# Attention blocks copied within SBUF by many small transfers of the load queue, and bias diagonals issued in other slots

## What is computed

```python
DIL_CONFIGS = ((128, 1), (512, 4), (2048, 16))   # window, dilation
HEADS_A, HEAD_DIM = 16, 64
qkv = (h @ w_qkv).reshape(B, T, N_GROUPS_A, 3, HEADS_A, HEAD_DIM)
for g, (window, dilation) in enumerate(DIL_CONFIGS):
    o, l = dilated_group_attention(qkv[:, :, g, 0], qkv[:, :, g, 1], qkv[:, :, g, 2],
                                   window, dilation, rel_table)
    ...
alpha = jax.nn.softmax(jnp.stack(lses, axis=0), axis=0)
o = jnp.sum(alpha[..., None] * jnp.stack(outs, axis=0), axis=0)
return o.reshape(B, T, D_MODEL) @ w_o
```

## Time and profile before

| | us |
|---|---|
| median of 3 runs | 1636.84 |
| the 3 runs | 1634.02 to 1636.91 |
| the profiled execution | 1637.76 |
| its span, first to last instruction | 1635.8 |
| mean granted TensorE clock | 0.986 |
| PE busy | 1590.2 (97%) |

### The profile page before, as it was taken

How to read it: one execution, slowest core, us unless ns; L and a number is a source line. 1 busy time by engine, 2 the same in 40 slices (tenths; PEclk the granted TensorE clock), 3 DMA queues, 4 the chain that set the end, 5 groups by cost and what they waited for, 6 DMA issues and landing times.

```text
span 1635.8 us, 21746 instructions
## 1 busy us (share of the span) xinstructions
PE 1590.2 (97%) x8034; PEld 1305.4 (80%) x8034; DVE 919.4 (56%) x1585; ACT 591.5 (36%) x1064; POOL 143.2 (9%) x208
## 2 busy tenths in 40 slices
PE   9999899899899999999999999999999999999998
PEld 7878678687688878888888887888878888888887
DVE  5456365464565774444545576776776353545565
ACT  5314233133133432222223345666653222222344
POOL 2020120211201110000000110000020000000111
PEclk9999899999999999999999999999999999999999
DMA  5574574755744333333333333233223333333332
GB/s 162 149 213 129 152 200 119 205 137 164 191 128 137 112 88 93 91 103 90 102 91 102 107 100 104 68 99 99 59 84 94 103 91 102 93 100 92 101 105 75
DMA packets 309980, 189.48 MB, mean 116 GB/s; under 512 B 33786, under 2 KB 297523, under 8 KB 309923
## 3 DMA queue, kind: packets, MB, share of 16 engines
q1 hardware_dynamic: 300112, 158.61, 33.9%
q0 software_dynamic: 9552, 30.08, 6.7%
q10 hardware_dynamic: 258, 0.04, 0.0%
HBM read 171.79 MB, written 25.28 MB: 120 GB/s over the span
## 4 chain that ended last, share of the span: by engine, by line
PE 87%; DMA 5%; SPq 2%; DVE 2%; POOL 1%; ACT 1%; issue 1%; ACTq 0%; POOLq 0%; DVEq 0%
PE unit_out L1704 24%; PE unit_out L1705 23%; PE unit_out L1706 23%; DMA w_raw<-in_a_w_qkv_dram 5%; SPq L747 2%; PE attn L1852 2%; POOL sumsq L912 1%; DVE w_lo L1238 1%; PE attn L2100 1%; PE turned L1780 1%; PE unit_out L1871 1%; PE unit_out L1872 1%; PE unit_out L1873 1%; PE logits L1704 1%; ACT w_hi L930 1%
## 5 line engine op out<-in xcount | busy, mean ns | idle before, releaser
L1704 PE MATMUL unit_out<-act_hi,w_hi 128*128 128x512 f32 x1849 | 732.1, 396 | 32.2 <-DVE w_lo L1238 30.7
L1706 PE MATMUL unit_out<-act_hi,w_lo 128*128 128x512 f32 x1849 | 723.4, 391 | 0.0
L1705 PE MATMUL unit_out<-act_lo,w_hi 128*128 128x512 f32 x1849 | 723.2, 391 | 0.0
L930 ACT ACTIVATE w_hi<-w_raw 128x1024 fp32r<-128x1024 f32 (+3 forms) x256 | 271.0, 1058 | 508.3 <-PE unit_out L1706 352.3
L1704 PEld LDWEIGHTS unit_out<-act_hi,w_hi 128*128 128x128 f32 x1849 | 350.6, 190 | 111.4 <-DVE w_lo L1238 36.8
L1706 PEld LDWEIGHTS unit_out<-act_hi,w_lo 128*128 128x128 f32 x1849 | 350.2, 189 | 73.8
L1705 PEld LDWEIGHTS unit_out<-act_lo,w_hi 128*128 128x128 f32 x1849 | 350.7, 190 | 70.4 <-issue 0.2
L1238 DVE TENSOR_TENSOR w_lo<-w_raw,w_hi 128x1024 fp32r<-128x1024 f32 (+3 forms) x256 | 319.7, 1249 | 146.2 <-ACT w_hi L930 145.9
L912 POOL TENSOR_TENSOR sumsq<-sumsq,square 128x512 f32<-128x512 f32 x41 | 57.8, 1411 | 1057.9 <-ACT square L958 1056.2
L1100 ACT ACTIVATE act_hi<-hidden 128x512 fp32r<-128x512 f32 x64 | 40.5, 633 | 243.4 <-DVE hidden L1502 243.4
L1499 DVE TENSOR_TENSOR scaled<-unit_out,rstd 128x512 f32<-128x512 f32 x62 | 42.8, 690 | 67.7 <-PE unit_out L1706 67.7
(11 more groups left out here) (297 smaller groups left out, 1388.5 us busy)
## 6 DMA issues: line engine op xcount, KB each, us to landing
w_raw<-in_w_ff_dram SPq DMA_DIRECT2D x128, 512.0 KB, 4.0
w_raw<-in_a_w_qkv_dram SPq DMA_DIRECT2D x56, 512.0 KB, 4.3
turned_blocks<-blocks POOLq DMA_DIRECT2D x28, 512.0 KB, 5.4
probs<-turned_blocks POOLq DMA_DIRECT2D x112, 128.0 KB, 4.1
w_raw<-in_b_w_qkv_dram SPq DMA_DIRECT2D x24, 512.0 KB, 4.9
w_raw<-in_a_w_qkv_dram SPq DMA_DIRECT2D x32, 256.0 KB, 3.9
w_raw<-in_w_ple_gate_dram SPq DMA_DIRECT2D x16, 512.0 KB, 3.9
bias_tiles_b<-bias_vectors SPq DMA_DIRECT2D x16, 256.0 KB, 5.1
```

What stands on the lines that cost most here:

```text
L930: sc.activation(weights_of(u)[0][:, 0:width, :], w_raw[par][:, 0:width, :], ACT.Copy).then_inc(hi_done, 1)
L1704: te.matmul(bank, w_k[0], hi, start=start, stop=False)
L1705: te.matmul(bank, w_k[0], lo, start=False, stop=False)
L1706: return te.matmul(bank, w_k[1], hi, start=False, stop=stop)
```

## The change

The tensor `turned_blocks` and POOL's loop go. In their place SP issues, for each phase, 16 transfers straight from `blocks` to `probs[ph]`, each of 32 rows x 256 floats (32 KB), with one wait for `blocks_ready` ahead of them (`spread_blocks`). They stand behind the loads of slots 6, 7, 8 and of slot 0 of the next step; the last of these in step 7 is behind the first load of `w_o`, which is therefore issued within the loop (`load_out_slab`). PE waits for 16 x 16 instead of 16 x 4 on `probs_landed`. The ten bias diagonals of `expand_a` are issued by head: five behind slot 4, five behind slot 5. `expand_b` stands in slots 2, 3 and 5.

```diff
+EXPAND_AT = {4: (0,), 5: (1,)}
+SPREAD_BEHIND = {6: 0, 7: 1, 8: 2, 0: 3}
-TILES_B_AT = [A_UNITS * step + slot for step in range(1, A_PAIRS) for slot in (0, 4, 8)][:HEADS]
+TILES_B_AT = [A_UNITS * step + slot for step in range(1, A_PAIRS) for slot in (2, 3, 5)][:HEADS]
...
-            def expand_a(pair):
+            def expand_a(pair, halves=(0, 1)):
...
-                for h in (2 * pair, 2 * pair + 1):
+                for h in [2 * pair + half for half in halves]:
...
-            for u in range(2, A_PAIRS * A_UNITS):
-                load_a(At(u // A_UNITS), At(u), u % A_UNITS)
+            def spread_blocks(step, n):
+
+                ph = A_TURN_ORDER[n]
+                sp.wait_ge(blocks_ready, A_ITEMS * (step - 1) + n + 1)
+                for i, j in itertools.product(range(NT), range(NT)):
+                    sp.dma_start(turned_order(probs[ph][j * SUB:(j + 1) * SUB, :])[:, i, :],
+                                 turned_order(blocks[i * SUB:(i + 1) * SUB, ph, :])[:, j, :]
+                                 ).then_inc(probs_landed[ph], 16)
+
+            for u in range(2, A_PAIRS * A_UNITS + 1):
+                if u < A_PAIRS * A_UNITS:
+                    load_a(At(u // A_UNITS), At(u), u % A_UNITS)
+                else:
+                    load_out_slab(U_AO, 0, a_w_o[0], u - U_AO)
+                slot = u % A_UNITS
+                step = u // A_UNITS - (slot == 0)
+                if slot in SPREAD_BEHIND and step > 0:
+                    spread_blocks(step, SPREAD_BEHIND[slot])
+                if u >= A_PAIRS * A_UNITS:
+                    continue
...
-                if u == 8 or u > A_UNITS and u % A_UNITS == 6 and u // A_UNITS < A_PAIRS - 1:
-                    expand_a(u // A_UNITS + 1)
+                if u == 8:
+                    expand_a(1)
+                if u > A_UNITS and u % A_UNITS in EXPAND_AT and u // A_UNITS < A_PAIRS - 1:
+                    expand_a(u // A_UNITS + 1, EXPAND_AT[u % A_UNITS])
...
-            for n in range(A_ITEMS * (A_PAIRS - 1)):
-                ph = A_TURN_ORDER[n % A_ITEMS]
-                pool.wait_ge(blocks_ready, n + 1)
-                pool.dma_start(blocks_d.ap()[ph], blocks[:, ph, :]).then_inc(blocks_stored, 16)
-                pool.wait_ge(blocks_stored, 16 * (n + 1))
-                for j in range(NT):
-                    pool.dma_start(turned_order(probs[ph][j * SUB:(j + 1) * SUB, :]),
-                                   blocks_d.ap()[ph].rearrange("(i k) (j c) -> k j i c", i=NT, j=NT)[:, j]
-                                   ).then_inc(probs_landed[ph], 16)
...
-                            wait(te, probs_landed[ph], s.times(16 * NT))
+                            wait(te, probs_landed[ph], s.times(16 * NT * NT))
```

More of the change, by code:

```diff
@@ L349, in build @@
         tiles_b = nc.dram_tensor("bias_tiles_b", (HEADS, P, T), F32, kind="Internal")
-        blocks_d = nc.dram_tensor("turned_blocks", (A_ITEMS, P, 2 * T), F32, kind="Internal")
         unit_out = [ps(f"unit_out{i}", [P, T]) for i in range(2)]
@@ L616, in build @@
         blocks_ready = sem("blocks_ready")
-        blocks_stored = sem("blocks_stored")
         probs_landed = [sem(f"probs_landed{i}") for i in range(A_ITEMS)]
@@ L776, in expand_b, with load_out_slab @@
                                      [[VEC, HEADS], [-1, P // HEADS], [1, T]])).then_inc(tiles_b_ready, 16)
-            for u in range(2, A_PAIRS * A_UNITS):
-                load_a(At(u // A_UNITS), At(u), u % A_UNITS)
+            def load_out_slab(first, layer, w_o, n):
+                load(At(first + n), w_o.rearrange("(k p) c -> p k c", p=P)[:, 0:KC - LATE[layer], n * P:(n + 1) * P])
+            def spread_blocks(step, n):
[16 more added lines that the diff above has]
+                    continue
                 if u == 3:
@@ L786, in _, with load_out @@
                     load_bias_a(u // A_UNITS)
-                if u == 8 or u > A_UNITS and u % A_UNITS == 6 and u // A_UNITS < A_PAIRS - 1:
-                    expand_a(u // A_UNITS + 1)
+                if u == 8:
+                    expand_a(1)
+                if u > A_UNITS and u % A_UNITS in EXPAND_AT and u // A_UNITS < A_PAIRS - 1:
+                    expand_a(u // A_UNITS + 1, EXPAND_AT[u % A_UNITS])
                 if u in TILES_B_AT:
                     expand_b(TILES_B_AT.index(u))
-            def load_out(first, layer, w_o):
+            def load_out(first, layer, w_o, done=0):
                 late = LATE[layer]
                 view = w_o.rearrange("(k p) c -> p k c", p=P)
-                for n in range(KC):
-                    load(At(first + n), view[:, 0:KC - late, n * P:(n + 1) * P])
+                for n in range(done, KC):
+                    load_out_slab(first, layer, w_o, n)
                 for i in range(late):
@@ L822, in load_gate @@
                                      ).then_inc(proj_raw_ready[par], 16)
-            load_out(U_AO, 0, a_w_o[0])
+            load_out(U_AO, 0, a_w_o[0], 1)
             sp.wait_ge(logits_done, ITEMS_A)
```

## The result

The changed kernel takes 1702.8 us (median of 4, 1701.45 to 1704.84) against 1635.9 of the kernel before (median of 4): a ratio of 1.0411, interval 1.0393 to 1.0429. The forecast was 1599 with a range of 1589 to 1638. The case that came true is rival C, SP as the bound, and it cost more than the 1671 given for it.

A forecast was written before the change was run, and what follows sets the result against it. PE was bound by six waits for weight loads issued late behind ten bias diagonals. 1637.8 - 45.4 (waits gone) + 7 (copies on SP) = 1599.4, with the median 0.9 lower: 1599 us, range 1589 to 1638.

The forecast's parts named there:

- rival C: SP becomes the bound; fourth phase's copies land 9.0 us late per step at pitch 0.60; 1671 us, chance 0.17.
- What bounds the kernel: PE, steps 1 to 6: six waits for late weight loads cost 45.4 us, 30.7 idle and 14.7 low clock.
- Diagonals split: Five diagonals behind slot 4, five behind slot 5: all six waits gone, -45.4 us; other bound about -13.
- Copies: Sixteen SP issues per phase at pitch 0.475 us; PE waits 1.0 us at the values product, seven times: +7 us.
- The upper bound of 0.60: Copy issue pitch on SP taken from the diagonals, instead of 0.475; would make PE wait 9.0 us a step.
- The working that went with it: SP falls behind 2.1 us per phase; step 7's last copies land at 516.0, wanted at 515.0; waiting begins at pitch 0.46.
- Low clock: Behind each PE wait the clock drops to 1.2 GHz, costing 2.4 us per wait beyond the idle time.
- The wait for `blocks_ready` on SP: Holds SP for nothing, since DVE transposes each phase just ahead of the `w_lo` that allows the preceding load.
- Up to 2 us of lag from the diagonals: If diagonals still hold SP when slot 6 is due, up to 2 us more per step, +12 us.
- The rules of the Trainium skill that speak against the change: Under 64 KB mostly overhead; more issuing engines save just issue time, which the change gives up, sized by the pitch.
- 33 us for sixteen copies: Time of a phase's copies run one after another by the skill page's fit; the prediction held that rows speak against it.

The follow-up runs named there:

- e1: Kernel before the change with only the diagonals split over slots 4 and 5 and layer-1 bias tiles in slots 2, 3, 5; blocks still over DRAM; 1602.3 us.
- e8: Changed kernel with POOL issuing all 16 copies per phase, ten diagonals back in slot 6 and bias tiles in slots 0, 4, 8; 1595.1 us.
- e5: Changed kernel with phases' copies varied: 32x256, 32x64 and 16x256 within SBUF, 32x256 from DRAM; only issue times read; one run, 1681.6 us.
- e7: Changed kernel with copies replaced by 128x64 and 1x256 within SBUF, 32x256 SBUF to DRAM and DRAM to DRAM; only issue times read; one run, 1691.3 us.
- e3: Changed kernel with all 16 copies of a phase issued by POOL, none by SP, slot moves kept; 1594.0 us.
- e6: Changed kernel with 8 of a phase's 16 copies issued by SP and 8 by POOL; 1592.2 us.
- e10: Changed kernel with 10 of a phase's 16 copies issued by SP and 6 by POOL; 1592.9 us.
- e9: Changed kernel with 12 of a phase's 16 copies issued by SP and 4 by POOL; 1631.4 us.

## Why the prediction was wrong, by its steps

**What bounds the kernel: right.** Six waits for a late load, 45.4 us with the clock behind them (45.46 by its rows). 1637.8 less 45.4 is 1592.4; the kernels without any such wait take 1592.2 and 1592.9.

**Diagonals split: right.** e1 has none of the six waits (it moves the bias tiles too). The working by the few engines they drain through was not tested by itself; e8 shows that the blocks' traffic beside them was the other half of the cause. The prediction names its share but gives it no price, and counts no gain for the direct copy by itself; with POOL as the issuer that copy alone takes away all but 2.2 us of the waits.

**Copies: this term failed, by its price.** I took 0.475 us for the pitch, from a two-dimensional load from DRAM of the same 32 KB. It measures 0.63. The size and shape that made that row look nearest do not set the price of a copy (e5, e7). What sets that row apart is that it crosses from DRAM to SBUF, and the copies do not. The upper bound of 0.60, from the diagonals, was the row of the right kind (both ends on one side), and I set it aside with the argument that they have DRAM at both ends. The load behind sixteen copies costs 0.58 to issue too, where the prediction has 0.42.

**The working that went with it: right in form.** Its threshold was a pitch of 0.46 at 16 copies, which is 7.8 us for a load and its copies. At a pitch of 0.63 that is 11 copies; the runs put it between 10 and 12. In step 7 SP's rows give 43.4 us from the load of slot 6 (534.57) to the last copy (578.0). PE allows 33.6 less 1.9 of landing, so the last copy is 11.7 us late instead of 1.0. Seven of these are 82 us; PE was measured idle for 76.2. The prediction also says that the loads bear the lag. At this price they do not: the waits for `w_lo` are 31.6 of the 76.2 us.

**Low clock: right in size, its number of times missed.** Seven steps, from the scores of step 1 to those of the drain, take 520.6 us in the changed kernel:

```profile
73.78 1.09 PE logits L1844 x16
...
594.33 1.09 PE logits L1844 x16
```

and 411.3 in e8:

```profile
73.28 1.09 PE logits L1854 x16
...
484.54 1.09 PE logits L1854 x16
```

The difference is 109.3 us. Of these 74.0 are idle (44.6 and 31.6, less the 2.2 that PE waits in e8). The other 35.3 are put down to the low clock, 2.5 for each of the 14 waits of over 2 us; the forecast had 2.4 each. Rival C reckoned with one wait per step and got 1671. A late SP makes two of them, one at the products for the last copies and one at a unit whose load is late, and each lowers the clock anew.

**The wait for `blocks_ready` on SP: right.** It held nothing: the copies follow their load without a gap in the timeline above.

**Up to 2 us of lag from the diagonals: about right.** In step 2 the load of slot 6 went out at 166.64, 0.7 us after it was allowed (164.72 and 1.18 for its `w_lo`), and the sixteen copies behind it took 11.6 us where those of the next phase took 10.1. That is 2.2 us in all, far too little to explain the loss.

**The rules of the Trainium skill that speak against the change.** That issuing from several engines only saves issue time ("DMA: Bandwidth & Descriptors", section "Issuing engines are not separate DMA queues") was cited as exactly what the change gives up. The rows agree: the 109 us between e3 and the changed kernel come from where the same 448 copies are issued. In each step 64 issues take 40 us of SP. The prediction's other figure, 33 us for sixteen copies, takes a fit that this page gives for transfers issued by POOL and applies it to SP; no run shows it for either, since sixteen copies took about 10 us on SP and 8 us on POOL, with landings of 1.9 and 2.5 us that overlap.

## What to carry to other kernels

Price a queue by what it must issue between two deadlines, not by the bytes: here ten copies a phase on SP cost nothing and twelve cost 39 us. For a transfer that the trace does not have, take the row whose two ends are of the same kind and which stands in a run of its like, and let the unfavourable row decide when the margin is thin. When a change carries two edits, ask what each is worth alone: here the slot moves gain about 2.0%, the direct copy from POOL 2.5%, and only the choice of SP as the issuer lost 4%. The lowest median is that of e6, with 8 copies on SP and 8 on POOL, 1592.2 us (2.7% faster than before). The intervals of e3, e8 and e10 overlap with its own, so these runs do not tell the four apart, and e3 or e8, with all copies on POOL, are the simpler kernels.

## What was not expected of the hardware

- In a run of sixteen equal transfers, an issue on SP costs 0.59 us when both ends are in SBUF or both in DRAM and 0.42 us when they differ (e5, e7). Within SBUF this held for 1 to 128 rows and 1 to 32 KB; the other kinds were tried at 32 x 256 only.
- The price of an issue depends on what was issued just ahead of it: the same weight load costs 0.37, 0.42 or 0.58 us (e7).
- POOL issues the same copy in 0.50 us, faster than SP (e3).
- Waits of PE of 2.1 to 4.2 us brought the clock to its lower level six times out of seven (e9), and waits of 2.4 to 7.3 us all fourteen times (the changed kernel). The low clock cost about 2.5 us per wait on top of it in the changed kernel, where the prediction read 2.4 from the kernel before.
